# Scores of each head's first query tile in one matmul over k's high and low part, with the addition on VectorE

## The reference

```
def hybrid_layer(x, attend, g_pre, w_in, g_sgu, w_sp, b_sp, w_out, g_post):
    h = rms_norm(x, g_pre)
    z = h @ w_in                          # q, k, v, gate, u, v_s, gate
    ...
    att = attend(q, k, v)
    gm, v_rows = gmlp_branch(u, vs, g_sgu, w_sp, b_sp)
    mix = jnp.concatenate([att * jax.nn.silu(ga), gm * jax.nn.silu(gg)], axis=-1)
    y = x + rms_norm(mix @ w_out, g_post)
    return y, k, v, v_rows

# attend, for the prompt
    s_own = jnp.einsum('bkgqd,bknd->bkgqn', q, k_own).astype(jnp.float32) * scale
    s_own = jnp.where(kpos[None, :] <= qpos[:, None], s_own, -jnp.inf)
    p = jax.nn.softmax(jnp.concatenate([s_sel, s_own], axis=-1), axis=-1)
```

## Time and profile before

| | |
|---|---|
| median of 3 runs | 276.45 us (276.37 to 276.78) |
| the profiled execution | 276.48 us |
| its span, from the first to the last instruction | 274.8 us |
| TensorE busy | 267.4 us, 97% |
| VectorE busy | 190.8 us, 69% |
| ScalarE busy | 167.2 us, 61% |
| GpSimd busy | 85.1 us, 31% |

### The profile page before, as it was taken

How to read it: one execution, slowest core, us unless ns; L and a number is a source line. 1 busy time by engine, 2 the same in 40 slices (tenths; PEclk the granted TensorE clock), 3 DMA queues, 4 the chain that set the end, 5 groups by cost and what they waited for, 6 DMA issues and landing times.

```text
span 274.8 us, 6135 instructions
## 1 busy us (share of the span) xinstructions
PE 267.4 (97%) x2127; PEld 235.8 (86%) x2127; DVE 190.8 (69%) x491; ACT 167.2 (61%) x387; POOL 85.1 (31%) x100
## 2 busy tenths in 40 slices
PE   7999999999999999999999999999999999999992
PEld 2799998998997888999788999998999976668892
DVE  4795896599835446857667877877967894818772
ACT  5974569531693323196989677787776644537621
POOL 4576604310302032324143973534251410000000
PEclk9999999999999999999999999999999999999998
DMA  7999997469898978604482318013028204040053
GB/s 242 320 254 219 215 249 144 144 180 276 232 313 232 312 233 280 220 0 156 140 247 85 67 19 263 1 35 120 0 67 327 89 1 153 10 145 0 21 191 115
DMA packets 31026, 43.39 MB, mean 158 GB/s; under 512 B 3043, under 2 KB 23523, under 8 KB 30996
## 3 DMA queue, kind: packets, MB, share of 16 engines
q1 hardware_dynamic: 27266, 29.76, 38.1%
q0 software_dynamic: 3728, 13.24, 16.0%
q10 hardware_dynamic: 2, 0.00, 0.0%
HBM read 39.59 MB, written 3.41 MB: 156 GB/s over the span
## 4 chain that ended last, share of the span: by engine, by line
PE 82%; ACT 10%; DVE 5%; issue 2%; DVEq 0%; POOL 0%; ACTq 0%; POOLq 0%
PE Z L1521 13%; PE Z L1522 12%; PE Z L1526 12%; PE T L1438 4%; PE O L1598 3%; PE S L1563 3%; PE O L1662 2%; ACT probs L976 2%; PE Z L1476 2%; PE S L1478 2%; PE S L1477 2%; PE S L1476 2%; PE Z L1478 2%; PE Z L1477 2%; PE S L1637 2%
## 5 line engine op out<-in xcount | busy, mean ns | idle before, releaser
L1521 PE MATMUL Z<-act_hi,w_hi 128*128 128x288 f32 (+1 forms) x344 | 89.7, 293 | 0.4 <-ACT zvs L900 0.3
L1522 PE MATMUL Z<-act_lo,w_hi 128*128 128x288 f32 (+1 forms) x344 | 88.1, 288 | 0.0
L1521 PEld LDWEIGHTS Z<-act_hi,w_hi 128*128 128x128 f32 x344 | 64.7, 188 | 2.7 <-issue 1.7
L1522 PEld LDWEIGHTS Z<-act_lo,w_hi 128*128 128x128 f32 x344 | 64.8, 188 | 0.0
L711 POOL TENSOR_TENSOR w_lo<-w_raw,w_hi 128x1024 fp32r<-128x1024 f32 x16 | 38.3, 2396 | 55.3 <-ACT w_hi L823 55.3
L1526 PE MATMUL Z<-act_hi,w_lo 128*128 128x256 f32 (+1 forms) x336 | 48.9, 288 | 0.0
L1526 PEld LDWEIGHTS Z<-act_hi,w_lo 128*128 128x128 f32 x336 | 44.9, 188 | 0.0
L823 ACT ACTIVATE w_hi<-w_raw 128x1024 fp32r<-128x1024 f32 x32 | 33.6, 1052 | 15.0 <-DMA w_raw<-in_w_out 10.0
L1070 DVE TENSOR_TENSOR w_lo<-w_raw,w_hi 128x1024 fp32r<-128x1024 f32 x15 | 18.3, 1224 | 16.2 <-ACT w_hi L823 16.2
L976 ACT ACTIVATE probs<-probs,nmax 128x128 f32<-128x128 f32 (+3 forms) x32 | 17.7, 555 | 12.6 <-DVE nmax L1312 12.5
L1197 DVE STREAM_TRANSPOSE kT<-k_ring 128x1024 f32<-128x1024 f32 x16 | 19.8, 1235 | 0.5 <-PE S L1563 0.2
(11 more groups left out here) (279 smaller groups left out, 556.1 us busy)
## 6 DMA issues: line engine op xcount, KB each, us to landing
w_raw<-in_w_in POOLq DMA_DIRECT2D x10, 1024.0 KB, 7.8
k_ring<-in_cache_k SPq DMA_DIRECT2D x64, 128.0 KB, 4.8
v_ring<-in_cache_v SPq DMA_DIRECT2D x64, 128.0 KB, 3.2
w_raw<-in_w_out SPq DMA_DIRECT2D x8, 512.0 KB, 4.4
x_sb<-in_x_prompt SPq DMA_DIRECT2D x4, 512.0 KB, 4.7
w_raw<-in_w_in SPq DMA_DIRECT2D x4, 512.0 KB, 7.2
x_res<-in_x_prompt SPq DMA_DIRECT2D x4, 512.0 KB, 5.3
out<-y_sb SPq DMA_DIRECT2D x8, 256.0 KB, 2.1
```

The lines of the kernel that those rows point to most:

```text
L1521: mm(out, wh[:, k, :], act_hi[:, k, cols], start=(k == 0), stop=False)
L1522: mm(out, wh[:, k, :], act_lo[:, k, cols], start=False, stop=False)
```

## The change

For units with i=0 the two matmuls of a head (256 columns over `k_hi`, then 256 over `k_lo` on top of it) become one matmul of 256 columns: 128 keys of the high part and 128 of the low part side by side. For this the two tiles are allocated as one, `k_both`, at the same addresses. The two halves of the scores are added on VectorE: first the mask is added to the high half, into `probs` (a `tensor_tensor` with a `link`), then the custom instruction adds the low half to that, with the same negation and minimum. All other units are as before.

```
-        k_hi = place("k_hi", [P, KVH, SEQ], f32r, R_Q + 16384)
-        k_lo = place("k_lo", [P, KVH, SEQ], f32r, R_Q + 24576)
+        k_both = place("k_both", [P, 2, KVH, SEQ], f32r, R_Q + 16384)
+        k_hi, k_lo = k_both[:, 0, :, :], k_both[:, 1, :, :]
...
                     for g in range(2):
                         dve.wait_ge(psc, 2 * u + g + 1)
+                        if keys == P:
+                            part = probs[:, u % 2, g, 0:P]
+                            link(nc.vector.tensor_tensor(part, S[:, g * 512:g * 512 + P], causal[:, SEQ - P:SEQ], ALU.add))
+                            nc.vector.tensor_tensor_reduce(part, S[:, g * 512 + P:g * 512 + 2 * P], part,
+                                                           -1.0, -4 * NEG, ALU.add, ALU.min, accum_out=nmax[:, u % 2, g:g + 1]).then_inc(p_masked, 1)
+                            continue
                         nc.vector.tensor_tensor_reduce(probs[:, u % 2, g, 0:keys], S[:, g * 512:g * 512 + keys], causal[:, SEQ - keys:SEQ],
                                                        -1.0, -4 * NEG, ALU.add, ALU.min, accum_out=nmax[:, u % 2, g:g + 1]).then_inc(p_masked, 1)
...
                         q = q_st[:, 2 * kvh + g, i * P:(i + 1) * P]
+                        if i == 0:
+
+                            mm(out, q, k_both[:, :, kvh, 0:P], start=True, stop=True).then_inc(psc, 1)
+                            continue
                         mm(out, q, k_hi[:, kvh, 0:keys], start=True, stop=False)
                         mm(out, q, k_lo[:, kvh, 0:keys], start=False, stop=True).then_inc(psc, 1)
```

## The result

The change is slower by 0.4%: 277.66 us median of 22 runs beside 276.39 us of the kernel before (22 runs), ratio 1.0042 with an interval of 1.0028 to 1.0056, that is 0.8 to 1.55 us more. One of the 22 runs of the change took 292.19 us at a mean granted clock of 0.851; it is not in the ratio, and without it the median is 277.63. Forecast were 277.27 us, +0.82, in a range of 276.6 to 277.65: the 277.66 lie 0.01 above its upper end, the 277.63 inside.

What follows compares the result with a forecast made beforehand. TensorE and the loop over VectorE and ScalarE were taken as neck and neck. Saving 0.94 us, all lost in waits; late 0.54 at u=11 plus 0.28 at u=12: 276.45 + 0.82 = 277.27 us, range 276.6 to 277.65.

Steps and rivals of the forecast that it cites:

- the loop over VectorE and ScalarE: Mask, exp, pT_hi, scaling, o_tmp, output sum, next mask: neck and neck with TensorE, lengthened by the change, delay reaching the end.
- TensorE's saving: On TensorE, 8 matmuls of 256 columns go at 0.1175 us each: 0.94 us, 0.235 per unit, all lost in waits.
- u=0: First i=0 unit: the loop is caught up by the mask of u=2, which waits for TensorE; nothing is left.
- The price of a unit: Additions on VectorE put pT_hi at m+1.55 instead of m+1.13, m being VectorE's arrival at the unit: 0.42 us per unit.
- The lower price: An addition costs only 0.21 from start to start, no wait: 0.22 us per unit, +0.22 in all, 276.7.
- u=8 and PTR u=11: Loop without slack up to the transposes of u=11: 0.12 + 0.42 = 0.54 us late, load at 190.27 instead of 189.73.
- the 0.12 of u=4: pT_hi 0.35 us late at u=4, of which 0.23 is hidden at the copies L1278; 0.12 goes on.
- u=12 and SP 0's bank: Loop 0.96 us late at sp_sum, bank free at 198.22; second transpose load of u=12 waits 0.28 more.
- The time around the span: Time of a run outside the profiled span: 1.7 us, added to the 274.8 us span.
- The first rival: TensorE sets the time, the loop doesn't: the 0.94 us saving stays, 275.5; chance 0.10, including half of it.
- The second rival: SP 0's bank in time, or 0.1 to 0.3 us hidden: +0.2 to +0.54; chance 0.18 with the cheap end.
- The third: Rival: the matmul's operand in two runs streams at half rate, nothing saved, still 277.27; no chance of its own.

Runs made afterwards that it cites:

- e1: The change with one matmul but no additions (the mask takes the high half only, the low part is left out): 276.11 us, ratio 0.9978 to the kernel before.
- e9: Kernel before with both matmuls kept and only VectorE's additions, the second instruction reading the scores from PSUM: 277.72 us, ratio 1.0033.
- e12: Kernel before with the whole change at u=4 alone: 276.89 us, ratio 1.0013.
- e6: Kernel before with the whole change at u=8 alone: 277.32 us, ratio 1.0034.
- e4: The changed kernel with the layer norm product LNM on VectorE moved from ahead of the mask to behind the gate: 276.22 us, ratio 0.999 to the kernel before.
- e5: The same changed kernel run again beside other kernels: 277.59 us, ratio 1.0038 to the kernel before.
- e8: Kernel before with both matmuls of an i=0 head cut to 128 columns, nothing added on VectorE: 276.35 us, ratio 0.9992.
- e7: Kernel before with the whole change at u=12 alone: 276.89 us, ratio 1.0008.
- e3: Kernel before with the layer norm product LNM on VectorE moved from ahead of the mask to behind the gate: 275.61 us, ratio 0.9966.
- e10: e3 with SP 0 also moved behind the transposes and value product of its step: 276.95 us, ratio 1.0006 to the kernel before.
- e11: e4 with SP 0 also moved behind the transposes and value product of its step: 279.06 us, ratio 1.006 to the kernel before.
- e2: Kernel before with both matmuls kept, the mask added first, then the custom instruction adding zeros out of `causal`, both operands in SBUF: 284.5 us, ratio 1.0286.

## Why the prediction was right

The mechanism was right: the loop over VectorE and ScalarE sets the end. Forecast +0.82; the traces show +0.78 and +0.73 from the first scores to the end. Step by step, times after from the zero 128.11 against those before from 127.69:

- **TensorE's saving, 0.94, forecast as all lost.** e1 and e9 show this with one exception: the change keeps 0.22 of it. The step on **u=0** ("Nothing is left of it") failed. The mask of u=2 waits for TensorE's scores, so when these come 0.2 earlier, the loop behind them does too. VectorE at u=2 before and after:

```profile
138.09 0.56 DVE L1312 CUSTOM_DVE_ANT_0 probs<-S,causal 128x384 f32<-128x384 f32 x1 [2.03 <-PE S L1638]
...
138.31 0.56 DVE L1318 CUSTOM_DVE_ANT_0 probs<-S,causal 128x384 f32<-128x384 f32 x1 [1.82 <-PE S L1648]
```

From the zeros that is 10.40 and 10.20 us. At u=4 VectorE is free for the unit 0.19 earlier (150.41 - 128.11 = 22.30; before 149.98 + 0.20 - 127.69 = 22.49). e12, which saves nothing at u=0, comes there at 22.47 and shows what the step would have given without this: +0.13 for u=4, forecast 0.12. In the change, u=4 ends at +0.03 and -0.02. The saving of u=8 was lost at PTR u=7 already and not, as forecast, at u=11.
- **The price of a unit, 0.42.** pT_hi at m+1.59 instead of the forecast m+1.55, at u=8 and u=12 (192.45 and 194.04). Against before it is 0.46. The rows follow each other as forecast, each by about 0.01 longer: mask 0.32 behind the addition, second addition together with the read, exp 0.04 behind it. The group of L1315 has a mean of 292 ns and that of L1314 285; the 280 of the earlier trace rows was a good neighbour. The lower price is not what the trace shows: an instruction that waits for the one before it starts 0.32 after that one's start, one that doesn't 0.21.
- **u=8 and PTR u=11, forecast +0.54.** The load stands at 190.58 - 128.11 = 62.47, before 62.04: +0.43, since the 0.12 of u=4 were not there. The unit's own price came through nearly whole, as in e6 (+0.44).
- **u=12 and SP 0's bank, forecast 0.28 more.** sp_sum starts at 197.85 - 128.11 = 69.74, before 68.84: +0.90, forecast 0.96. The bank's release took longer than the 0.04 put into the sum: sp_sum ends at 198.54 and the load starts at 198.65, 0.11. These two errors cancel, and the load, forecast +0.82, stands +0.83 (70.54; before about 197.40 - 127.69 = 69.71). That it is this bank is shown by e4's view of waits and by the chain.
- **What follows is late by one amount**: +0.87 at u=14, +0.83 at u=15.
- **The time around the span, taken as 1.7 us before and after.** This failed too. A run's time less its span is 1.73 us in the mean of the runs of before beside e5 (1.67 to 1.79), and 1.93 in the change (1.75 to 2.07), 1.89 in e5. e1 and e8, without additions, have 1.73 and 1.74; e9, the additions alone, has 1.92; e6, e7 and e12, with additions at one unit, 1.78 to 1.82. So the additions bring about 0.2 us that no trace holds. Why they do, no run shows.

That the forecast meets the traces within 0.1 us is partly luck. Three units cost 0.04 more each and the bank's release 0.07 more, together 0.19, and u=0's saving brought 0.19 back.

The first rival (TensorE sets the time, 275.5) fell with e9 and e1: without the additions a little under half of its gain shows, with them a quarter. But e4 shows the point from which it starts to be true: where the loop has slack, the change is ahead by 0.6 up to u=12. The second rival (bank in time, or 0.1 to 0.3 us hidden) came true at u=4 in part, by way of u=0's saving, but the bank came late and took as much back. The third (the operand in two runs at half rate) is out. The score matmuls of u=12 in the changed kernel's timeline on TensorE:

```profile
189.22 0.39 PE L1645 MATMUL S<-k_both,q_st 128*128 128x256 f32 x2
```

Both together take 0.39, one alone 0.28 as in the earlier trace rows, so they start 0.11 apart; and e1 keeps 0.45 behind u=4, near the 2 x 0.235 of two units.

**What stays open.** The medians moved by 1.27 us in the first set and 1.11 in e5's; the lowest runs by 0.90 (277.06 and 276.16). The interval of the ratio reaches down to 0.5 to 0.8 us and so holds the 0.73 to 0.78 of the traces, but the middle of it is some 0.3 us above. About 0.2 of this is the time around the span; in e5's set the medians of the spans alone differ by 0.90. For e4 the whole interval (-0.75 to +0.19 us) lies above its trace's -0.99, and the 0.2 don't close that gap. The time up to the first scores varies by 1.2 us between profiled executions of code that is the same up to there; whether the changed kernels are there later more often was not tried.

**A version that beats both** is e3, before with LNM behind the gate: 0.9966 (0.9951 to 0.9982) of before. The change on top of it (e4) adds nothing that the times show: its trace is 0.10 us shorter from the first scores, its median 0.6 us longer.

## What to carry to other kernels

A busy share of 97% doesn't make an engine the bound: idle time ahead of one load (0.55 us here) and a chain that stays on two other engines for 29 us said that the saving would be waited away. To size the loss, follow the delay through each wait that it meets and take off the slack that each of them has. Moving work from the fullest engine to one in the loop that feeds it costs what it adds between the start of that engine's work and the start of the consumer (0.46 us per unit here, for two additions of 0.28), and gives little until the loop has slack (0.22 of 0.94 us here). A buffer shared by two steps (T's banks) is a wait of its own: shifting the one user ahead or back moves the wait, and it can come out larger, as in e10 and e11.

## What the runs showed of the hardware

- VectorE's custom instruction with both operands in SBUF took 2.31 to 2.36 us in three units of e2 while GpSimd's L711 (2.39 to 2.40 us) ran, and 0.29 away from it; with one operand in PSUM (the change, e9) it took 0.29 in every unit. The Trainium skill (SBUF — State Buffer, section on who interferes with whom) has a rule for this: VectorE reads a second SBUF input through an interface that it shares with GpSimd, and the later of the two waits for the whole instruction of the other. The trace agrees: VectorE's instruction started 0.18 to 0.22 behind GpSimd's and ended 0.14 to 0.15 behind its end.
- A score matmul with its weight load takes 0.113 us at 128 columns and 0.1175 at 256.
- Behind e11's wait of 1.9 us TensorE's granted clock fell: 0.97 in the mean of 195 to 200 us, in which it was busy for 3.06 of the 5 us, and 0.69 in the next 5. Matmuls of 256 columns at 201.78, 201.99 and 202.21 stood 0.21 apart, those at 199.43 and 199.55 still 0.12. Behind e10's wait of 1.1 us (3.89 of the 5 us busy) it stayed at 1.00.
- In the change at u=8 two VectorE instructions of 128x128 stood 0.32 us apart, start to start, where the second waited for the first, and 0.21 where it didn't. At u=12, 0.11 us passed from the end of sp_sum on VectorE (198.54) to TensorE's load for the bank that it had freed (198.65).
